# A two-layer hybrid decoder trunk on one core: latent-attention heads with quadrant rotary products, values projected with time on partitions, and unrolled pairs

## The reference: what is computed

```python
def mla_attention(c_q, c_kv, k_rope, positions, g_cq, g_ckv, w_uq, w_ukv):
    q = (rms_norm(c_q, g_cq) @ w_uq).reshape(B_, L, MLA_HEADS, MLA_NOPE + MLA_ROPE)
    q = jnp.concatenate([q[..., :MLA_NOPE], rope(q[..., MLA_NOPE:], positions)], axis=-1)
    kv = (rms_norm(c_kv, g_ckv) @ w_ukv).reshape(B_, L, MLA_HEADS, MLA_NOPE + MLA_V)
    kr = rope(k_rope[:, :, None, :], positions)
    k = jnp.concatenate([kv[..., :MLA_NOPE], jnp.broadcast_to(kr, (B_, L, MLA_HEADS, MLA_ROPE))], axis=-1)
    v = kv[..., MLA_NOPE:]
    o = causal_block_attention(q, k, v, (MLA_NOPE + MLA_ROPE) ** -0.5)
```

## Time and profile before

| | |
|---|---|
| median of 3 runs | 2300.54 us (2298.49 to 2301.47) |
| the profiled execution's own time | 2301.95 us |
| its span, first to last instruction | 2300.3 us |
| PE busy | 2259.4 us (98% of the span) |
| DVE / ACT / POOL busy | 998.4 / 824.1 / 401.7 us |
| granted TensorE clock, mean | 0.996 |
| the latent stage, from its first product to the next line of OUT1A | 1852.0 to 1937.2 us |

### The profile page before, as it was taken

How to read it: one execution, slowest core, us unless ns; L and a number is a source line. 1 busy time by engine, 2 the same in 40 slices (tenths; PEclk the granted TensorE clock), 3 DMA queues, 4 the chain that set the end, 5 groups by cost and what they waited for, 6 DMA issues and landing times.

```text
span 2300.3 us, 30844 instructions
## 1 busy us (share of the span) xinstructions
PE 2259.4 (98%) x11901; PEld 1834.5 (80%) x11901; DVE 998.4 (43%) x1865; ACT 824.1 (36%) x1457; POOL 401.7 (17%) x691
## 2 busy tenths in 40 slices
PE   7999999999999999999999999999999999999998
PEld 7888887787788877888788778888887866778886
DVE  4632454444432256643353441441222255666534
ACT  6533233333332534422332233222232444545323
POOL 1626112222221012100010001100000253221100
PEclk9999999999999999999999999999999999999999
DMA  7645434444445346563343446445443664454532
GB/s 284 203 140 139 128 108 129 120 130 121 115 116 194 103 154 203 172 216 100 130 134 121 136 138 226 128 134 162 139 128 102 206 208 154 154 180 151 206 104 92
DMA packets 166923, 345.65 MB, mean 150 GB/s; under 512 B 21535, under 2 KB 32111, under 8 KB 164355
## 3 DMA queue, kind: packets, MB, share of 16 engines
q1 hardware_dynamic: 106832, 188.51, 26.9%
q0 software_dynamic: 31248, 98.44, 13.5%
q10 hardware_dynamic: 28707, 56.84, 6.8%
HBM read 279.89 MB, written 63.83 MB: 149 GB/s over the span
## 4 chain that ended last, share of the span: by engine, by line
PE 96%; DVE 1%; issue 1%; ACT 1%; DMA 0%; DVEq 0%; SPq 0%; ACTq 0%
PE PS L241 79%; PE PS L1699 3%; PE PS L2365 2%; PE PS L1688 2%; PE PS L291 1%; PE PS L558 1%; PE PS L1122 1%; PE PS L2262 1%; PE PS L2225 1%; PE PS L1448 1%; PE PS L2014 1%; PE PS L1870 1%; PE PS L2258 1%; PE PS L1895 1%; PE PS L1118 1%
## 5 line engine op out<-in xcount | busy, mean ns | idle before, releaser
L241 PE MATMUL PS<-A,wsp 128*128 128x512 f32 (+2 forms) x5184 | 1160.4, 384 | 1.5 <-ACT stage L344 1.2
L241 PEld LDWEIGHTS PS<-A,wsp 128*128 128x128 f32 (+1 forms) x5184 | 941.9, 188 | 198.9 <-issue 8.8
L210 DVE TENSOR_TENSOR wsp<-wraw,wsp 128x1024 fp32r<-128x1024 f32 (+1 forms) x358 | 433.0, 1210 | 991.7 <-ACT wsp L203 990.5
L241 PE MATMUL PS<-wsp,A 128*128 128x512 f32 x2928 | 750.4, 401 | 4.2 <-DVE stage L1770 2.2
L203 ACT ACTIVATE wsp<-wraw 128x1024 fp32r<-128x1024 f32 (+1 forms) x358 | 372.2, 1042 | 912.1 <-PE PS L241 880.8
L241 PEld LDWEIGHTS PS<-wsp,A 128*128 128x128 f32 x2928 | 531.4, 189 | 105.0 <-issue 7.6
L344 ACT ACTIVATE stage<-PS 128x512 f32<-128x512 f32 (+1 forms) x150 | 87.1, 587 | 141.4 <-PE PS L241 136.8
L1735 ACT ACTIVATE S<-PS 128x256 f32<-128x256 f32 (+3 forms) x160 | 63.0, 394 | 127.4 <-PE PS L1688 126.6
L1699 PEld LDWEIGHTS PS<-S 128*128 128x128 f32 x640 | 93.6, 193 | 12.0 <-issue 2.4
L1743 ACT ACTIVATE S<-PS,stats 128x256 f32<-128x256 f32 (+3 forms) x160 | 74.7, 467 | 74.1 <-DVE stats L1780 61.9
L1699 PE MATMUL PS<-S 128*128 128x128 f32 x640 | 95.6, 276 | 1.2 <-issue 1.1
(11 more groups left out here) (342 smaller groups left out, 1731.5 us busy)
## 6 DMA issues: line engine op xcount, KB each, us to landing
wraw<-in_even_w_in_dram SPq DMA_DIRECT2D x112, 512.0 KB, 3.7
wraw<-in_odd_w_in_dram SPq DMA_DIRECT2D x88, 512.0 KB, 3.6
wraw<-in_w_out_dram SPq DMA_DIRECT2D x80, 512.0 KB, 3.8
wraw<-in_mem_w_kv_dram SPq DMA_DIRECT2D x32, 512.0 KB, 4.2
yO<-stage ACTq DMA_DIRECT2D x12, 1024.0 KB
yE<-stage ACTq DMA_DIRECT2D x10, 1024.0 KB
S<-yO POOLq DMA_DIRECT2D x36, 256.0 KB, 3.7
hA<-stage ACTq DMA_DIRECT2D x8, 1024.0 KB
```

The source lines that it names most:

```text
L210: nc.vector.tensor_tensor(wsp[:, q, 1, :, 0:j["cols"]], wraw[:, q, :, 0:j["cols"]], wsp[:, q, 0, :, 0:j["cols"]].bitcast(F32), ALU.subtrac ...
L241: mm = nc.tensor.matmul(dst, lhs, rhs, start=(s == 0 and kk == 0 and i == 0), stop=(s == j["spc"] - 1 and kk == 1 and i == 2))
```

## The change

`UKV` is read so that its even chunks are the keys of four heads and its odd ones the values of four heads, the latter with time on partitions (`turned=(1, 3)`), stored in a new tensor `vM`; the keys alone go to `kvD`. Each UKV slot is loaded by two DMAs of 128-column pieces instead of one DMA. The transposes of the values on PE and their copies on ACT are gone; POOL loads values from `vM` by a DMA of their own, on which `pe_values` waits. The rotary queries of a pair are laid out so that each block of 128 queries has its first 64 in partitions 0 to 63 and its other 64 in partitions 64 to 127, and the rotary product becomes two products of 64 by 64 by w. This takes 12 DMAs per pair in pieces of 64 columns instead of 6 of whole rows, tables of half the width (`pool_half_tables`), and sums of 256 columns on all partitions. All engines have the pairs written out. POOL's order is new, before the stage and in it.

```diff
-        UKV = job("UKV", a["mla_w_ukv"][0], 4, 4, hi=36, lo=12)
+        UKV = job("UKV", a["mla_w_ukv"][0], 4, 4, hi=36, lo=12, turned=(1, 3))
@@ sp_slot
+            if j is UKV:
+                heads = j["w"].rearrange("p k (h e d) -> p k h e d", e=2, d=P)
+                for kk in range(2):
+                    sp.dma_start(wraw[:, q, kk, :].rearrange("p (h d) -> p h d", d=P),
+                                 heads[:, 2 * s + kk, 4 * (c // 2):4 * (c // 2) + 4, c % 2, :]).then_inc(w_loaded[q], 16)
+                return
@@ store_rows
+                if j is UKV:
+                    return vM[:, c // 2 * COLS:(c // 2 + 1) * COLS].rearrange("(f p) d -> p f d", p=P)
@@ pe_values; pe_vt and act_vt and their calls are removed
-                if t.vt:
-                    pe.wait_ge(t.vte, num(b, 2, h0 + 1 + t.v0))
+                pe.wait_ge(v_in[r], num(b, 16, 16 * (h0 // 2) + 16 - 16 * t.b0))
@@
-        def run_pairs(eng, t, body, unrolled=False):
+        def run_pairs(eng, t, body, unrolled=True):
@@ pool_mla
             gate(0, (t.b0, 2, -1), (t.b0, 2, -2 * t.b0))
-            pool_sum(pool, qrS, 1)
-            with pool.Fori(t.b0 + 1, t.b0 + t.pairs) as b:
+            for b in range(t.b0 + 1, t.b0 + t.pairs):
                 h = num(b, 2, -2 * t.b0)
-                pool_rotary_load(pool, h)
+                pool_rotary_turn(pool, h)
                 gate(1, (b, 2, -2), (b, 2, -1 - 2 * t.b0))
                 wait(pool, t.sc, b, t.upp, -t.uph)
-                wait(pool, t.vtp, b, 2, t.v0 - 1)
                 mla_qkv(pool, h, 0, t.ld[0])
-                pool_rotary_turn(pool, h)
-                pool_sum(pool, qrS, 0)
+                pool_sum(pool, 0)
                 wait(pool, t.sc, b, t.upp, 0)
-                wait(pool, t.vtp, b, 2, t.v0)
-                mla_qkv(pool, num(b, 2, 1 - 2 * t.b0), 1, t.ld[1])
-                pool_sum(pool, qrS, 1)
+                mla_qkv(pool, h + 1, 1, t.ld[1])
+                pool_sum(pool, 1)
+                wait(pool, t.pv, b, t.upp, -t.uph)
+                mla_v(pool, h, 0)
+                if h + 2 < t.heads:
+                    pool_rotary_load(pool, h + 2)
                 gate(0, (b, 2, -1), (b, 2, -2 * t.b0))
+                wait(pool, t.pv, b, t.upp, 0)
+                mla_v(pool, h + 1, 1)
@@ mla_score
-                nc.tensor.matmul(bank[:, 0:w], q[:, i * P:i * P + P], k[:, 0:w], start=True, stop=False)
                 if x % 4 == 0:
                     pe.wait_ge(rope_ok, num(b, 2, x // 4 + 3 - 2 * MLA.b0))
-                half = slice(64 * r, 64 * r + 64)
-                nc.tensor.matmul(bank[:, 0:w], qrS[half, i * P:i * P + P], krS[half, 0:w], start=False, stop=False)
+                nc.tensor.matmul(bank[:, 0:w], q[:, i * P:i * P + P], k[:, 0:w], start=True, stop=False)
+                for e in range(2):
+                    half = slice(64 * e, 64 * e + 64)
+                    nc.tensor.matmul(bank[half, 0:w], qrS[half, r, i * 64:i * 64 + 64], krS[half, 0:w], start=False, stop=False)
                 causal_mask(bank, w).then_inc(MLA.sc, 1)
@@ new functions of POOL
+        def pool_rotary_queries(pool, h):
+            heads = quD[ds(h * 192, 384), :].rearrange("(r q) (i e u) -> q r i e u", r=2, i=4, e=2)
+            for e in range(2):
+                src = lambda o, n: heads[P + o:P + o + n, :, :, e, :]
+                for r in range(2):
+                    pool.dma_start(qa4[64 * e:64 * e + 64, r], src(0, 64)[:, r]).then_inc(rope_ld, 16)
+                    pool.dma_start(qb4[64 * e:64 * e + 32, r], src(32, 32)[:, r]).then_inc(rope_ld, 16)
+                    pool.dma_start(qb4[64 * e + 32:64 * e + 64, r], src(0, 32)[:, r]).then_inc(rope_ld, 16)
+        def pool_half_tables(pool):
+            for e in range(2):
+                half = slice(64 * e, 64 * e + 64)
+                for k, tab in enumerate((cosR, sinR)):
+                    nc.gpsimd.tensor_copy(turn2[half, k, :].rearrange("p (i u) -> p i u", i=4),
+                                          tab[half, :].rearrange("p (i e u) -> p i e u", i=4, e=2)[:, :, e, :]).then_inc(half_tab, 1)
+            pool.wait_ge(half_tab, 4)
+        def pool_sum(pool, r):
+            nc.gpsimd.tensor_tensor(qrS[:, r, :], qa3[:, r, :], qb3[:, r, :], ALU.add).then_inc(rope_ok, 1)
+        def mla_v(pool, h, r):
+            pool.dma_start(MLA.v[r][:, 0, :, :], vM[:, ds(h * P, P)].rearrange("(j p) d -> p j d", p=P)).then_inc(v_in[r], 16)
@@ POOL's program ahead of the stage
             pool_turn(pool, 0)
-            pool_sum(pool, krS, 0)
-            pool_sum(pool, krS, 1)
+            pool_sum_keys(pool, 0)
+            pool_sum_keys(pool, 1)
+            pool_half_tables(pool)
             pool.wait_ge(stored, 16 * (UKV["stored0"] + 1))
             pool_rotary_load(pool, 0)
             pool_rotary_turn(pool, 0)
-            pool_sum(pool, qrS, 0)
+            pool_sum(pool, 0)
+            pool_sum(pool, 1)
+            pool_rotary_load(pool, 2)
             mla_qkv(pool, 0, 0, MLA.ld[0])
             pool.wait_ge(w1_used, 8)
             mla_qkv(pool, 1, 1, MLA.ld[1])
+            pool.wait_ge(stored, 16 * (UKV["stored0"] + 2))
+            mla_v(pool, 0, 0)
+            mla_v(pool, 1, 1)
             pool.wait_ge(stored, 16 * OUT1A["stored0"])
             pool_mla(pool, MLA)
```

More of the change, by code:

```diff
@@ L193, in act_slot @@
                 pairs = list(range(O1["slot0"] + 5 * O1["spc"], O1["slot0"] + 7 * O1["spc"])) + list(range(O2["slot0"], O2["slot0"] + O2["spc"]))
+                pairs += list(range(UKV["slot0"], UKV["slot0"] + 4 * UKV["spc"]))
                 halves = len([m for m in pairs if m <= n and m % RAW == n % RAW])
@@ L375, in store_rows @@
             if name == "UKV":
-                return rows(kvD[c * COLS:(c + 1) * COLS, :])
+                return rows(kvD[c // 2 * COLS:(c // 2 + 1) * COLS, :])
             return {"E2": yF.rearrange("g r t -> (g r) t"), "O2": yO[6656:6744, :]}[name]
@@ L1450, in pe_values @@
             mm.then_inc(t.pv, 1)
[L1452 to L1477, removed]
         def dve_finish(dve, t, b, h):
@@ L1511, in body @@
                         pe_scores(pe, t, b, x)
-                        pe_vt(pe, t, b, x)
                     if (x >= LT or not first) and not (tail and x >= LT):
@@ L1914, in build @@
         quD = dram("quD", (1536, T))
-        kvD = dram("kvD", (2048, T))
+        kvD = dram("kvD", (1024, T))
+        vM = dram("vM", (T, 1024))
         cmpD = dram("cmpD", (2, P, NPAD + P))
@@ L2277, in build, with pool_rotary_keys @@
         rope_ld, rope_c = sem("rope_ld"), sem("rope_c")
-        def pool_rotary(pool, src, s_):
+        qa4, qb4 = [v.rearrange("p (r i u) -> p r i u", r=2, i=4) for v in (qa, qb)]
+        qa3, qb3 = [v.rearrange("p (r t) -> p r t", r=2) for v in (qa, qb)]
+        def pool_rotary_keys(pool):
+            src = lambda o, n: yO[6656 + o:6656 + o + n, :]
             for e in range(2):
-                pool.dma_start(qa[64 * e:64 * e + 64, :], src(e, 0, 64)).then_inc(s_, 16)
-                pool.dma_start(qb[64 * e:64 * e + 32, :], src(e, 32, 32)).then_inc(s_, 16)
-                pool.dma_start(qb[64 * e + 32:64 * e + 64, :], src(e, 0, 32)).then_inc(s_, 16)
+                pool.dma_start(qa[64 * e:64 * e + 64, :], src(0, 64)).then_inc(kr_in, 16)
+                pool.dma_start(qb[64 * e:64 * e + 32, :], src(32, 32)).then_inc(kr_in, 16)
+                pool.dma_start(qb[64 * e + 32:64 * e + 64, :], src(0, 32)).then_inc(kr_in, 16)
+        def pool_rotary_queries(pool, h):
[13 more added lines that the diff above has]
+            pool.wait_ge(half_tab, 4)
         def pool_rope_start(pool):
@@ L2288, in pool_rope_start @@
             pool.dma_start(posrI, a["positions"].broadcast_to([P, T])).then_inc(rope_in, 16)
-            pool_rotary(pool, lambda e, o, n: yO[6656 + o:6656 + o + n, :], kr_in)
+            pool_rotary_keys(pool)
         def dve_rope(dve):
@@ L2319, in pool_turn @@
         def pool_turn(pool, n):
-            nc.gpsimd.tensor_tensor(qa, qa, cosR, ALU.mult).then_inc(rope_c, 1)
-            nc.gpsimd.tensor_tensor(qb, qb, sinR, ALU.mult).then_inc(rope_c, 1)
+            if isinstance(n, int) and n == 0:
+                nc.gpsimd.tensor_tensor(qa, qa, cosR, ALU.mult).then_inc(rope_c, 1)
+                nc.gpsimd.tensor_tensor(qb, qb, sinR, ALU.mult).then_inc(rope_c, 1)
+            else:
+                by = [turn2[:, k, :].unsqueeze(1).broadcast_to([P, 2, 256]) for k in range(2)]
+                nc.gpsimd.tensor_tensor(qa3, qa3, by[0], ALU.mult).then_inc(rope_c, 1)
+                nc.gpsimd.tensor_tensor(qb3, qb3, by[1], ALU.mult).then_inc(rope_c, 1)
@@ L2323, in pool_turn, with pool_sum_keys @@
             pool.wait_ge(rope_c, n * 2 + 2)
-        def pool_sum(pool, dst, e):
+        def pool_sum_keys(pool, e):
             half = slice(64 * e, 64 * e + 64)
-            nc.gpsimd.tensor_tensor(dst[half, :], qa[half, :], qb[half, :], ALU.add).then_inc(rope_ok, 1)
```

(18 more changed lines are left out.)

11 lines of the change are left out of this document (5 added, 6 removed).

## The result

The change makes the kernel slower by 0.25 to 0.31% (ratio and medians): median 2306.53 us (2304.14 to 2308.4, 10 runs) against 2299.49 us (2298.12 to 2303.88, 10 runs) of the kernel before on the same chip, ratio 1.0025 with a 95% interval of 1.0016 to 1.0033. The forecast was 2304.1 us and a chance of 0.42 for this side, 0.46 for no change that can be told. The mechanism forecast (late start of the stage) is there; it is larger than forecast.

A forecast was written before the change was run, and what follows sets the result against it. PE was taken to bound the kernel (96% of the wait chain). Terms -4.5 (heads), +5.7 (start), +1.8 (clock), +0.6 (loop) sum to +3.6 us: median 2304.1 us against 2300.54, 8-in-10 range 2296.5 to 2311.

The forecast's parts named there:

- late start of the stage: Latent stage's start: POOL's loads delay head 0's k, so PE starts at 1857.7 instead of 1852.0, +5.7 us.
- the landing: Stage start: head 0's k, once issued, lands 3.0 us later in quiet queues; 3.6 us taken because a store is in flight.
- 8 us of slack in the old order: Stage start: argument for the rival that the loads are in time, as the old POOL order left 8 us spare.
- 12 more issues: Stage start: argument against the rival that loads are in time, 12 more load issues than before at well-known rates.
- The clock: Stage start: PE, idle some 6 us, loses its clock, +1.8 us (bounds 0 and 3.4).
- Steady heads: Pairs two to four: values 0.46 and quadrants 0.20 us less PE work per head, -4.0 us over six heads.
- the rival of serial quadrants: Rotary products: the quadrants run one behind the other, 17 us lost, 2321 us (half overlapped 2313); chance 5%.
- First pair: Stage's first pair: 1.3 us less PE work, but waits for ACT mostly lengthen; -0.5 us (bounds 0 and -1.3).
- Loop: Pair borders: POOL's chain leaves k's load no slack, 0.3 us at each of two borders, +0.6 us (bounds 0 and 4).
- Loads in time: Rival at stage start: late by under 2 us, no idle PE, full clock, 2297 us; chance 17%.
- POOL can't keep pace: Rival in the loop: POOL becomes the bound; with 2 us at each of two borders, 2308 us; chance 15%.
- The change gives more than I count: Rival: start on time and the first pair's 1.3 us too, or clock dips in SEQ1 shift; 2294 us; chance 8%.

The follow-up runs named there:

- e6: Changed kernel with six of the second pair's twelve rotary loads moved behind q, k and values of heads 0 and 1: 2299.64 us, ratio to before 0.9995.
- e3: Changed kernel plus 36 unread matmuls of 512 columns on PE just ahead of the stage: 2303.84 us, ratio to before 1.0014.
- e9: Kernel with q and k first at start and in loop, plus a POOL wait putting the turn behind DVE's finish: 2296.97 us, ratio to before 0.9987.
- e5: Changed kernel with the old rotary product, whole tables, sums and six loads per pair: 2299.3 us, ratio to before 0.9997.
- e4: Kernel before with only the values turned in the projection and loaded by their own DMA, POOL's pairs written out: 2298.14 us, ratio 0.9994.
- e1: Changed kernel with the second pair's twelve rotary loads moved behind q, k and v of heads 0 and 1: 2297.05 us, ratio to before 0.9987.
- e2: e1 with q and k of a pair's first head also ahead of the rotary turn in the loop: 2297.21 us, ratio to before 0.9992.
- e10: e1 with a POOL wait putting the turn behind DVE's finish, turn still ahead of q and k: 2298.63 us, ratio to before 0.9998.
- e8: Kernel before with only PE's, ACT's and DVE's pairs written out instead of looped: 2301.27 us, ratio 1.0007.

## Why the prediction was right in its mechanism and short in its size

**The start, step by step.** Forecast and measured:

| step | forecast | measured |
|---|---|---|
| keys' second sum ends | 1828.3 | 1829.14 |
| half tables, four copies | 1.6 | 1.54 |
| result to first load | 0.57 | 1.13 |
| twelve loads (first set) | 7.2 | 6.9 |
| landing, POOL idle | 4.0 | 3.40 |
| two products | 2.6 | 2.6 |
| two sums | 1.4 | 2.3 |
| to the second set, its twelve loads | 0.57 + 7.2 | 0.29 + 6.8 |
| k issued | 1854.1 | 1854.72 |
| from k's issue to PE's start | 3.6 | 5.8 (landing 5.5) |
| PE starts | 1857.7 | 1860.55 |

The chain on POOL came out within 0.6 us, as errors of both signs cancel. A sum of 128 by 256 takes 1.15 us here, not 0.7 (in the loop 0.74). **The step that failed is the landing**: "k lands 3.0 us later if the queues are quiet ... I take 3.6". They were not quiet: the DMA share is 0.87 over the idle stretch. What held k was, by the trace, the 1 MB store of the values and not the twelve small loads. Ten of these landed in about 2 us; from 1854 to 1857 the store's queue had 93.5% of the DMA engines' time and POOL's 6.6%, and what POOL issued from 1853.07 on came about 2 us late. In e6, where k was issued before the store moved, it landed in 3.2 us; in e3, behind the store again, in 6.1. No run takes the store away, so its price of some 2 us stays an estimate from these rows. I knew of the store ("in flight until 1856.58") and allowed 0.6 us for it. The 3.0 is also a figure of q: a load of k takes a median of 3.9 us in the loop of after. And the "8 us of slack in the old order" was counted with the quiet landing; before, head 0's k and v, issued at 1841.69, took 7.3 us, which leaves 3. (The rival's "12 more issues" ahead of k are 18: 24 against 6. The step list has them right.)

**Issues.** 64 rows in four pieces (256) cost 0.62 to 0.68 us, 32 rows in four (128) 0.55; forecast 0.72 and 0.54. The row that I used for 256 pieces was of 128 rows in two, so the number of pieces alone does not set the cost. The Trainium skill, DMA: Bandwidth & Descriptors, Anatomy of one DMA, calls descriptor generation small; by that the twelve would have taken an estimated 6.4 us. They took 6.8 to 6.9, between rule and row.

**The clock.** Forecast 1.8 of at most 3.4; e3 measures 2.5 to 2.7. The level fell as forecast; what I had wrong is the discount. I let part of the slower matmuls fall into the waits of the first pair, but the 5.5 us at half clock lie wholly in the first head, where PE has no waits (busy 5.45 of 5.50). The forecast's 6.4 us of idle time would hardly have been safe either, as 4.1 us were not in the earlier trace rows; the 3.0 us of e6 were.

**Steady heads.** Forecast 9.33, measured 9.36 (e9 has five such distances in a row). Quadrants 0.19 (e5; forecast 0.20, a pair at 128 keys 0.37 as forecast from the earlier trace rows), values 0.44 (e4; forecast 0.46). Six heads: -3.8 of -4.0. The quadrants do run side by side; the rival of serial quadrants is out.

**First pair.** With the clock's 2.5 taken out, +0.9 becomes -1.6. The kernels with full clock there have 19.59 us (e6), 19.58 (e1, with a wait of 0.29 for k), 19.13 (e2 and e10) and 18.74 (e3) against 20.28 of before: -0.7 to -1.5. The forecast -0.5 is low. The waits did not take most of what was saved: PE is idle 1.9 us in the first pair of e2, as in before.

**Loop.** Forecast 0.6, measured 1.3 (one stall of 1.00, the other heads up to 0.1 long). One head at a border is 1.16 us longer than a steady one, which is a sign that the prediction named for being wrong ("more than 1 us"). I had seen a slack of nil in the keys' load. Here too the landing was short: that k was issued 15.2 us after the pair's start (forecast 15.4 to 15.8) and took 4.7 us to land, not 3.0. What I had not seen is that POOL's turn and DVE's finish of a head hinder each other.

**The rivals.** "Loads in time" forecast 2297, and e1, where they are, measured 2297.05: its price was right and its condition not met. "POOL can't keep pace" asked for 2 us at each border; 1.0 at one came, a part of this rival. "The change gives more than I count" did not come. Pairs written out: nothing, e8. In all, start +7.65 (forecast 5.7), first pair and clock +0.9 (+1.3), later heads -2.5 (-3.4), upstream +0.9 (0): 6.9 against 3.6.

## What to carry to other kernels

When a queue's order puts loads for later in front of loads that are needed now, count the issues between them, and price the landing by what else moves at that moment: here the late k met a 1 MB store that the early k would have missed. A landing time is good only for its own transfer and its own traffic. Then see how long the engine that waits stands still, since its clock can go as well. The cure was one line: what PE needs first is issued first. When vector work on POOL is moved, look at DVE's own long instructions at the new place, as the loss shows up on PE two waits later with neither named.

## What the runs showed of the hardware that was not expected

- POOL and DVE block each other. DVE's subtraction from SBUF took 3.89 us instead of 0.69 in e2 (twice), the cast 3.10 instead of 0.52 in e1 (3.21 in e3 and e6), each lasting to 0.3 to 0.6 us behind POOL's two products; one wait that kept them apart (e9, e10) made both short. The Trainium skill, SBUF — State Buffer, Who interferes with whom, says that the two engines share a pair of ports which one of them locks for an instruction, so that the other stands still; the trace agrees, with these numbers. In e9 the issue of k at 1883.36 lies within the same subtraction and does not lengthen it. By the records in e2 the subtraction begins 0.8 us before POOL's product and would have ended before it; POOL's times are rough, and what held it that early stays open.
- The clock can fall behind short waits, and need not. In e4 2.3 us of idle time in four pieces within 10.4 us were followed by 6.8 us at 0.51, where the before kernel, with 1.9 us idle in its first pair, kept 1.00. e2 and e9 have the same four waits there (0.16, 0.16, 0.38 and 1.24 us in e2; none differs by over 0.01), yet e2 kept 1.00 and e9 had 3.4 us at 0.50. So the idle time alone does not decide it, and what does is open.
- A store of 1 MB held POOL's loads back almost wholly: 93.5% of the DMA engines' time went to its queue and 6.6% to POOL's for 3 us, and loads of 32 KB landed after 4.4 to 4.5 us instead of 2.0.
- A single wait of 3.0 us (e6) left the granted clock at its upper level of 2.4 GHz, one of 8.4 us (after) was followed by 5.5 us of work at 1.2 GHz.
